# Causal convolution of a two-block transformer: eight channel tiles over three engines in place of two

## What is computed, cut to the stage in question

```python
CONV_WIDTH = 31                                   # taps
u = hn @ w_pw1 + b_pw1                            # (256, 2048)
a, g = jnp.split(u, 2, axis=-1)
u = a * jax.nn.sigmoid(g)                         # (256, 1024)
u = lax.conv_general_dilated(u, w_dw[:, None, :], window_strides=(1,),
        padding=((CONV_WIDTH - 1, 0),), dimension_numbers=("NWC", "WIO", "NWC"),
        feature_group_count=D_MODEL) + b_dw       # one filter of 31 taps for each channel
u = jax.nn.silu(layernorm(u, ln_g, ln_b))
return u @ w_pw2 + b_pw2                          # (256, 1024), added to h
```

## Time and profile before

| | |
|---|---|
| median of 3 runs | 2400.33 us (2399.83 to 2401.45) |
| the profiled execution's own time | 2397.07 us |
| its span in the trace | 2395.2 us |
| granted TensorE clock | 0.995 |
| busy: TensorE / VectorE / ScalarE / GpSimd | 97% / 74% / 61% / 4% of the span |
| the convolution's taps, by the trace | 1716.7 to 1778.7 us after the start |

### The profile page before, as it was taken

The page is one execution under the profiler, slowest core; times in us unless marked ns, Lnnn a source line. Parts: engine busy times, 40 slices in busy tenths (PEclk is TensorE's granted clock), DMA queues, the critical chain, the costliest instruction groups (busy, mean ns, idle before and its releaser), DMA issues.

```text
span 2395.2 us, 30749 instructions
## 1 busy us (share of the span) xinstructions
PE 2327.5 (97%) x11626; PEld 1947.9 (81%) x11626; DVE 1765.0 (74%) x1697; ACT 1456.1 (61%) x1580; POOL 83.9 (4%) x115
## 2 busy tenths in 40 slices
PE   8999999989999999999999999999999999999998
PEld 7787887777888888888888888887778887778987
DVE  5676446667898989898999898898785456564456
ACT  5633444456777777777767776776674356554355
POOL 0000000006100000000000000000000000000000
PEclk9999999999999999999999999999999999999999
DMA  8206654428999999999999999998403546323542
GB/s 298 103 6 207 211 188 164 150 105 322 361 373 367 367 372 362 372 361 366 367 376 356 377 355 375 336 378 273 166 20 141 208 162 211 141 80 141 188 181 88
DMA packets 266569, 597.12 MB, mean 249 GB/s; under 512 B 8677, under 2 KB 40161, under 8 KB 265824
## 3 DMA queue, kind: packets, MB, share of 16 engines
q1 hardware_dynamic: 262512, 582.00, 66.5%
q0 software_dynamic: 3920, 13.66, 1.7%
q10 hardware_dynamic: 32, 0.02, 0.0%
HBM read 591.43 MB, written 4.19 MB: 249 GB/s over the span
## 4 chain that ended last, share of the span: by engine, by line
PE 79%; DVE 10%; ACT 5%; DMA 4%; issue 1%; ACTq 0%; DVEq 0%; SPq 0%
PE up L2277 15%; PE up L2279 15%; PE up L2278 14%; PE acc L2277 7%; PE acc L2279 7%; PE acc L2278 7%; DMA raw<-in_ffn_w 4%; DVE wl L1523 4%; ACT wh L848 3%; DVE arena L1982 2%; PE up L2939 1%; PE up L2941 1%; PE up L2940 1%; PE tp L2712 1%; PE tp L2251 1%
## 5 line engine op out<-in xcount | busy, mean ns | idle before, releaser
L1860 DVE TENSOR_TENSOR wl<-raw,wh 128x2048 fp32r<-128x2048 f32 x378 | 865.6, 2291 | 111.5 <-ACT wh L1122 108.2
L1122 ACT ACTIVATE wh<-raw 128x2048 fp32r<-128x2048 f32 x378 | 727.3, 1925 | 203.9 <-PE up L2279 107.1
L2277 PE MATMUL up<-wh,xTh 128*128 128x512 f32 x1664 | 661.3, 397 | 11.1 <-DVEq L2200 1.8
L2279 PE MATMUL up<-wh,xTl 128*128 128x512 f32 x1664 | 649.1, 390 | 0.0
L2278 PE MATMUL up<-wl,xTh 128*128 128x512 f32 x1664 | 648.0, 389 | 0.0
L1523 DVE TENSOR_TENSOR wl<-raw,wh 128x2048 fp32r<-128x2048 f32 x168 | 382.6, 2291 | 322.6 <-ACT wh L848 320.8
L848 ACT ACTIVATE wh<-raw 128x2048 fp32r<-128x2048 f32 x168 | 320.9, 1919 | 317.3 <-PE up L2279 120.7
L2277 PEld LDWEIGHTS up<-wh,xTh 128*128 128x128 f32 x1664 | 313.4, 188 | 80.9 <-issue 14.3
L2279 PEld LDWEIGHTS up<-wh,xTl 128*128 128x128 f32 x1664 | 312.9, 188 | 66.7
L2278 PEld LDWEIGHTS up<-wl,xTh 128*128 128x128 f32 x1664 | 313.7, 189 | 61.6 <-issue 0.5
L2277 PE MATMUL acc<-wh,hTh 128*128 128x512 f32 x816 | 319.3, 391 | 3.0 <-DVE hTl L1880 1.5
(11 more groups left out here) (413 smaller groups left out, 2219.0 us busy)
## 6 DMA issues: line engine op xcount, KB each, us to landing
raw<-in_moe_w_gate SPq DMA_DIRECT2D x126, 1024.0 KB, 6.7
raw<-in_moe_w_up SPq DMA_DIRECT2D x126, 1024.0 KB, 7.1
raw<-in_moe_w_down SPq DMA_DIRECT2D x126, 1024.0 KB, 6.3
raw<-in_ffn_w SPq DMA_DIRECT2D x32, 2048.0 KB, 8.4
raw<-in_hg_w_in SPq DMA_DIRECT2D x7, 2048.0 KB, 14.6
raw<-in_da_w_in SPq DMA_DIRECT2D x6, 2048.0 KB, 8.1
raw<-in_ffn_w_gate SPq DMA_DIRECT2D x11, 1024.0 KB, 6.8
raw<-in_ffn_w_up SPq DMA_DIRECT2D x11, 1024.0 KB, 11.1
```

Source lines behind the costliest of these rows:

```text
L1122: f(wh[:, x % SPLITS, :], raw[:, x % RAW, :], ACT.Copy).then_inc(moe["hi"], 1)
L1860: V.tensor_tensor(wl[:, x % SPLITS, :], raw[:, x % RAW, :], wh[:, x % SPLITS, :].bitcast(F32), ALU.subtract).then_inc(moe["lo"], 1)
L2277: mm(out, x_hi, w_hi, start=start, stop=False)
L2279: return mm(out, x_lo, w_hi, start=False, stop=stop)
```

## The change

GpSimd takes tiles 0 and 1, VectorE tiles 2, 3 and 4 and TensorE tiles 5, 6 and 7. GpSimd computes tap 0 with one tensor_scalar for each tile, and each further tap with a tensor_scalar (slice of uT times weight, into a scratch of 128x256, for which the idle tiles `lam` and `few_rows` serve) and a tensor_tensor (cT plus scratch). After the two tiles' scaled copies and after their additions it waits for them (`link`). These instructions stand in its queue between the load of the first bias and that of the second. VectorE's early taps are now of tiles 2 and 3 and wait for these. TensorE's first tile is 5, and it waits for it; tiles 6 and 7 follow after the last turn. The turn back and one load of SyncE, four units into the feed-forward layer, wait for GpSimd's `cv_pool` as well.

```diff
-    CV_DVE, CV_PE = [0, 1, 2, 4], [3, 5, 6, 7]
+    CV_POOL, CV_DVE, CV_PE = [0, 1], [2, 3, 4], [5, 6, 7]
@@ SyncE, at u == 3 of the feed-forward layer
                         sp.wait_ge(cv_dw, 1)
+                        sp.wait_ge(cv_pool, 1)
                         sp.wait_ge(cv_tap, CONV * len(CV_PE))
@@ GpSimd
             load_rows(t["conv_b_pw1_2"][0][0:D], t["conv_b_pw1_2"][0][D:2 * D])
+
+            pool.wait_ge(s_vecs, 2)
+            pool.wait_ge(s_Te, t_cv[1] + 1)
+            pool.wait_ge(cv_n, 3)
+            scaled = lam[:, 0:SEQ], few_rows[:, 0:SEQ]
+            for j in range(CONV):
+                for k in CV_POOL:
+                    src = uT[:, k, j:j + SEQ]
+                    if j == 0:
+                        ins = nc.gpsimd.tensor_scalar(cT[:, k, :], src, wdw[:, k, 0:1], rowcols[:, 0, k:k + 1], ALU.mult, ALU.add)
+                    else:
+                        ins = nc.gpsimd.tensor_scalar(scaled[k], src, wdw[:, k, j:j + 1], None, ALU.mult)
+                link(ins)
+                if j > 0:
+                    for k in CV_POOL:
+                        ins = nc.gpsimd.tensor_tensor(cT[:, k, :], cT[:, k, :], scaled[k], ALU.add)
+                    link(ins)
+            pool.sem_inc(cv_pool, 1)
             pool.wait_ge(s_rows_free, 5)
             load_rows(t["conv_b_pw2_2"][0])
             pool.wait_ge(s_ppe, 8)
@@ VectorE, after chunks 2 and 3
                 if c >= 2:
-                    dve.wait_ge(s_Te, t_cv[1] + 1)
+                    dve.wait_ge(s_Te, t_cv[3] + 1)
                     for j in range(EARLY * (c - 2), EARLY * (c - 1)):
                         tap(j, CV_DVE[0:2])
@@ TensorE
         def first_taps():
 
-            pe.wait_ge(s_Te, t_cv[3] + 1)
+            pe.wait_ge(s_Te, t_cv[5] + 1)
             taps(0)
 
         project(g_cv, t_cv, 4, T_cv, 2, enter_cv, before_last=first_taps)
-        pe.wait_ge(s_Te, t_cv[5] + 1)
-        taps(1)
         pe.wait_ge(s_Te, T_cback)
-        for i in range(2, len(CV_PE)):
+        for i in range(1, len(CV_PE)):
             taps(i)
         pe.wait_ge(cv_dw, 1)
+        pe.wait_ge(cv_pool, 1)
         pe.wait_ge(cv_sum, len(CV_PE))
```

More of the change, by code:

```diff
@@ L483, in _program @@
     cv_dw, cv_n = sem("conv_done"), sem("conv_normed")
+    cv_pool = sem("conv_pool_done")
     cv_diag, cv_tap, cv_sum = sem("conv_diagonals"), sem("conv_taps"), sem("conv_sums")
```

## The result

The changed kernel takes 2441.0 us (2439.22 to 2442.20), the kernel before 2400.3 us: a ratio of 1.0171, 95% interval [1.0156, 1.0187], 40.7 us slower. The forecast was 2428 us in a range of 2404 to 2452, slower. So the side and the range were right, and the central value was 13 us short. The profiled execution has 2440.02 us and a span of 2438.2.

A forecast was written before the change was run, and what follows sets the result against it. VectorE was taken to bound the stage, TensorE close behind. VectorE's 1766.5 us plus 35.7 of conflict and 1.5 of projection loss, then GpSimd's remainder and 1 us restart, moved the end 28 us: 2428 us, range 2404 to 2452.

The forecast's parts named there:

- The bound of before: In the convolution stage, VectorE's taps set the end at 1778.75 us, with TensorE 1 us behind; relieving one alone brings nothing.
- VectorE's and TensorE's parts: Undisturbed, with their smaller shares of the convolution's tiles, VectorE ends at 1766.5 us and TensorE's last sum at 1765.2 us.
- GpSimd's part alone: GpSimd's taps of tiles 0 and 1 without contention: 73 us from 1698.6 us, to 1771.6 us; upper end 89 us.
- The conflict: In the convolution, GpSimd's SBUF-reading instructions and VectorE's two-input ones block each other, each waiting for the other's.
- the hold: How long each GpSimd instruction delays a VectorE tap: 0.38 us, bounds 0.19 and 0.73.
- the pairing of each tap of VectorE with one instruction of GpSimd: From 1716.7 us, 100 remaining GpSimd instructions alternate one to one with VectorE's 90 taps, 2 multiplications and 2 splits.
- the sum: Stage total: VectorE late by 35.7 and 1.5 us, to 1803.7; GpSimd done at 1806.5; the kernel's end 28 us later.
- rival 2: GpSimd is shut out while VectorE's convolution taps run back to back: +48 us, 2449 us; chance 0.15.
- The signs: Expected in the stage's trace: GpSimd instructions 0.8 us or more apart, VectorE taps 0.7 to 0.9, both done near 1805.
- Rival 1: No conflict either way between GpSimd and VectorE in the convolution: 2393 us, 2409 with dearer additions; chance 0.17 with its variant.
- its second form: GpSimd waits for VectorE's convolution instructions but never holds them up, ending between 1767 and 1783 us; within the 0.17.
- The 1 us for TensorE's slow restart: At the turn back after the convolution, TensorE's transposes start slowly after idling, adding 1 us.

## Why the prediction was right, and where it was short

- The bound of before, the cover of the second bias's load, and the passage of the stage's end to the kernel's end: right. The stage grew by 40.4 us and the kernel by 40.7; the second bias is used at 1852.29 us, 30.9 us after the turn back, after the same wait as before.
- VectorE's and TensorE's parts: right. Undisturbed, VectorE ends at 1766.75 us (1766.5 forecast) and TensorE's products at 1764.91 us (1765.2 with the last sum), and the kernel without GpSimd's taps gains 11.4 us.
- GpSimd's part alone: the step that failed. The tensor_tensor was taken at 0.70 us and has 0.68 to 0.70; the link at 0.07 has 0.08 to 0.11. The tensor_scalar was taken at 0.43 us with 0.50 as its end; the two of the first tap start 0.5 us apart, but the sixty others have 0.90. The row of before in the earlier trace rows had one operation too, but 8 columns and 0.25 us. That the fixed part hides the price there is an estimate: (0.92 - 0.25) / 248 columns is 2.7 ns a column, 0.02 us for eight. 60 x 0.47 = 28 us are missing in this term, and GpSimd alone takes 103.3 us, not 73. Not even its upper end held: with 0.50 and 0.97 the same sum is 31 + 58.2 + 4.3 = 93.5 us (the 89 us stated there leave the tensor_scalar at 0.43).
- The conflict: both directions are as forecast, and so is nearly the hold, 0.27 to 0.28 us for each of GpSimd's instructions (0.38 forecast; 0.19 to 0.73 were the bounds). Two steps were wrong. The hold was taken as GpSimd's own time less 0.14 us, and it does not follow that time: it is the same with copies of 0.90 and of 0.46 us. And the pairing of each tap of VectorE with one instruction of GpSimd holds only with short copies; with long ones VectorE fits one and a half taps beside each, and the extra ones pass undisturbed.
- What the conflict costs the path: the sum made it 35 us of GpSimd's length. It is 6.4 us behind the taps and 10.4 us behind the splits. And since GpSimd ends last, what VectorE loses (18.8 us, ending at 107.0 instead of 88.1 us after the load) is off the path; in the forecast it was the path.
- So two errors offset each other: 30 us too little for the price, 18 too much for the conflict. That the forecast is only 13 us off, less than either error, is luck. The side did not need it, since 103.3 us alone already put GpSimd's end past the kernel before's. The range held because its upper end was set by GpSimd instructions that are long and hold VectorE up for all of it (0.73 us each), and by rival 2. They were long, but that is not how they cost the time. Its low side was loose too: the steps of the sum with a hold of 0.19 us lead to about 2410 us, not 2407.
- The signs: TensorE idles from 1767 us, many of VectorE's taps are marked longer than 0.48 us, and GpSimd's stand 3.77 / 4 = 0.94 us apart in the mean, as forecast. VectorE's are 0.64 apart, not 0.7 to 0.9, GpSimd's before 1716 us are 0.7 to 0.9 apart where no split holds them, not near 0.6, and the two don't end together near 1805 us but at 1787.4 and 1821.2. By its own last sign, GpSimd long at work after VectorE, the prediction would have called this rival 2; the sign was a bad one, as a slow GpSimd gives it too.
- The rule of the Trainium skill (SBUF — State Buffer, "Who interferes with whom") that two SBUF inputs of VectorE conflict with a GpSimd instruction that reads SBUF, and with none that only writes: the runs with PSUM sums and with memsets agree on both counts. That the holder keeps the port for its whole instruction agrees where a split holds it (a GpSimd instruction beside one takes 2.86 us). It does not agree where GpSimd holds it, if the instruction is what the trace shows: 3.77 us hold a tap of GpSimd, 3.40 us alone, and two taps of VectorE with three tiles, 2 x 1.31 us alone, together 6.0 us of work.
- Rival 1 (no conflict) and its 2393 us fall with both its price and its premise; its second form, in which GpSimd never holds VectorE up, falls with the fifty taps (31.82 against 22.75 us). Rival 2 (GpSimd shut out) falls by the trace: GpSimd gets its instructions done while VectorE's taps run back to back, 3.77 us for a tap instead of 3.40. Its 2449 us is near the result for another reason.
- The 1 us for TensorE's slow restart: 0.8 us.

## What to carry to other kernels

Before work goes to GpSimd, price it at its real size and in the exact form: a row of 8 columns shows only the fixed part, and the same multiplication took 0.90, 0.57 or 0.46 us from start to start, undisturbed, by how it was written. Beside a busy VectorE its instructions that read SBUF conflict with those of VectorE that read two tensors there; here a running sum kept in PSUM took the conflict of the taps away at no cost to VectorE. What that is worth is read from the engine that ends last: it was 5.9 us of the stage, though VectorE ended 17.8 us earlier. And here the division over three engines paid only when it was made in taps rather than tiles: the same idea was 1.7% slower at first and 0.2% faster once form, place and share were mended.

## What the runs showed of the hardware that I had not expected

- GpSimd's tensor_scalar on 128x256 float32 takes 0.92 us with one operation and 0.48 us with two (0.90 and 0.46 from start to start); with two tensors it takes 0.72 for an addition and 0.61 at best for a multiplication by a spread column (0.68 and 0.57 from start to start).
- A GpSimd instruction that reads SBUF holds up one of VectorE's two-tensor taps by 0.27 to 0.28 us in the mean, whether the copies take 0.92 or 0.48 us; a split of VectorE holds up GpSimd by some 2 us.
- VectorE's tensor_scalar with one tensor of SBUF conflicts with GpSimd as well, with its memsets too (0.45 to 0.48 us beside it instead of 0.31).
- VectorE's scalar_tensor_tensor with its sum in PSUM is as quick as with both in SBUF: 1.31 us for three tiles in both.
- TensorE's clock: after a wait of 3.18 us the granted clock of the next 4 us was 0.57 in the mean (1.2 GHz, and 2.4 again at the end), after 10.00 us it was 0.50, and after a wait of 1.95 us (the run without GpSimd's taps) it stayed at 1.00. But the run with memsets, with a wait of 2.06 us, started its transposes at 2.4 GHz and fell to 1.2 GHz on the way, so a short wait is no safe one:

```profile
1767.50:1769.00 1.50, 1.09 (x8) 0.86 (x8) 0.06 (x1) 0.78 (x3) 0.00 (x0) 0.95 0.00 0
1769.00:1771.00 2.00, 1.99 (x9) 1.99 (x10) 1.48 (x3) 1.05 (x2) 0.00 (x0) 0.50 0.00 0
```

Sixteen transposes took 3.7 us instead of 2.5 where the clock was down from their start, and 3.3 in the run with memsets. From the turn back to the product the loss was 0.8 to 0.9 us, and 0.3 in the run with memsets.
